# Two blocks on one core: narrower products in three passes, and the projections' first product begun inside the norms

## The reference, cut to what matters

```python
# block 1 (16 learned tokens in front: 1040 rows)
u = rms_norm(h, norm1_g)
a, bv, bg, q, k, v, fg, gates = split(u @ w_in)        # 256, 256, 256, 512, 512, 512, 8, 3*1024 columns
ya = pool_mixer(a) @ w_out_a                           # 256 deep
yb = conv_module(bv, bg) @ w_out_b                     # 256 deep
logf = log_sigmoid(fg + b_forget)                      # the "forget" product, 8 columns
yc = forgetting_attention(q, k, v, logf) @ w_out_c     # 512 deep
g = sigmoid(gates.reshape(B, L, 3, D))
merged = g[:, :, 0] * ya + g[:, :, 1] * yb + g[:, :, 2] * yc
h = h + merged @ w_o                                   # then a mixture of experts

# block 2
u = rms_norm(h, norm_mix_g)
x_rnn, g_rnn, q_c, kv_c, k_pe, gates = split(u @ w_in) # k_pe: 32 columns
xa = causal_conv(x_rnn)
r = sigmoid(blockwise(xa, wa) + ba); i = sigmoid(blockwise(xa, wx) + bx)   # four blocks of 256 x 256 each
ya = scan(a(r), b(i, xa)) * gelu(g_rnn)
yb = mla(q_c, kv_c, k_pe, positions)                   # latent attention
h = h + (gates_0 * ya + gates_1 * yb) @ w_out          # then another mixture of experts
```

## Time and profile before

| | before |
|---|---|
| runs (us) | 2941.87, 2947.04, 2951.19: median 2947.04 |
| the profiled execution | 2947.81; span of its trace 2946.0 |
| PE busy | 2662.0 us, 90% of the span, 12234 matmuls |
| DVE, ACT, POOL busy | 1487.1, 1113.0, 826.2 us (50%, 38%, 28%) |
| mean granted clock of PE | 0.954 |

### The profile page before, as it was taken

The page is one execution under the profiler, slowest core; times in us unless marked ns, Lnnn a source line. Parts: engine busy times, 40 slices in busy tenths (PEclk is TensorE's granted clock), DMA queues, the critical chain, the costliest instruction groups (busy, mean ns, idle before and its releaser), DMA issues. The chain is left out here.

```text
span 2946.0 us, 34212 instructions
## 1 busy us (share of the span) xinstructions
PE 2662.0 (90%) x12234; PEld 2032.9 (69%) x12234; DVE 1487.1 (50%) x1840; ACT 1113.0 (38%) x1461; POOL 826.2 (28%) x685
## 2 busy tenths in 40 slices
PE   4999899999999799958999799999999999699887
PEld 3899565776768677736777455557777868677665
DVE  4196343222223478855476544433542542678775
ACT  3011443000012277752344344441332232377775
POOL 1243332212112133412100233232333322144545
PEclk9999899999999799968899899999999999799999
DMA  3110112111105487842522232322111223598995
GB/s 95 30 51 22 33 43 58 41 50 43 43 18 184 168 290 235 277 127 82 214 65 65 75 85 73 74 74 81 43 42 50 57 88 125 193 326 301 325 316 195
DMA packets 209416, 350.52 MB, mean 119 GB/s; under 512 B 40376, under 2 KB 159496, under 8 KB 189608
## 3 DMA queue, kind: packets, MB, share of 16 engines
q1 hardware_dynamic: 191824, 315.60, 32.2%
q0 software_dynamic: 17280, 33.60, 4.9%
q10 hardware_dynamic: 216, 0.07, 0.0%
HBM read 326.80 MB, written 72.48 MB: 136 GB/s over the span
## 5 line engine op out<-in xcount | busy, mean ns | idle before, releaser
L2101 DVE TENSOR_TENSOR moe_run_w_low_up<-moe_run_w,moe_run_w_high_up 128x2048 fp32r<-128x2048 f32 x116 | 265.4, 2290 | 123.0 <-ACT moe_run_w_high_up L1934 122.7
L1934 ACT CAST moe_run_w_high_up<-moe_run_w 128x2048 fp32r<-128x2048 f32 x116 | 221.2, 1907 | 117.1 <-DMA moe_run_w<-w_gate 59.2
L1871 PE MATMUL moe_run_up<-moe_run_w_high_up,moe_run_xT_high 128*128 128x512 f32 x464 | 193.0, 416 | 21.0 <-issue 20.7
L1871 PE MATMUL moe_run_up<-moe_run_w_high_up,moe_run_xT_low 128*128 128x512 f32 x464 | 184.3, 397 | 0.0
L1871 PE MATMUL moe_run_up<-moe_run_w_low_up,moe_run_xT_high 128*128 128x512 f32 x464 | 184.2, 397 | 0.0
L1417 DVE TENSOR_TENSOR merge_gated<-merge_branch,merge_gate 128x512 f32<-128x512 f32 x48 | 33.2, 692 | 281.1 <-ACT merge_gate L1401 280.9
L1277 ACT ACTIVATE mla_probs<-mla_scores 128x512 f32<-128x512 f32 x192 | 94.1, 490 | 177.5 <-PE mla_scores L1209 91.8
L1401 ACT ACTIVATE merge_gate<-merge_gates 128x512 f32<-128x512 f32 x48 | 28.7, 598 | 348.0 <-PE merge_branch L122 348.0
L1222 PE MATMUL mla_out<-mla_probs,mla_v 128*65 128x512 f32 (+3 forms) x384 | 151.2, 489 | 0.0
L2101 DVE TENSOR_TENSOR moe_run_w_low_down<-moe_run_w,moe_run_w_high_down 128x2048 fp32r<-128x2048 f32 x58 | 132.4, 2282 | 0.0
L1296 DVE TENSOR_REDUCE mla_piece_max<-mla_max 128x1 f32<-128x512 f32 (+1 forms) x192 | 99.0, 550 | 62.8 <-PE mla_max L1181 42.9
(11 more groups left out here) (570 smaller groups left out, 7394.2 us busy)
## 6 DMA issues: line engine op xcount, KB each, us to landing
moe_run_w<-exp_w SPq DMA_DIRECT2D x72, 1024.0 KB
moe_run_w<-w_gate SPq DMA_DIRECT2D x34, 1024.0 KB
moe_run_w<-w_up SPq DMA_DIRECT2D x34, 1024.0 KB
moe_run_w<-w_down SPq DMA_DIRECT2D x34, 1024.0 KB
out_h<-x SPq DMA_DIRECT2D x16, 512.0 KB
v<-out_v SPq DMA_DIRECT2D x16, 512.0 KB, 2.9
mla_raw_q_then_weights<-w_in SPq DMA_DIRECT2D x16, 512.0 KB, 3.9
rnn_raw<-w_in SPq DMA_DIRECT2D x16, 512.0 KB
```

The lines of the kernel that those rows point to most:

```text
L1871: last = pe.matmul(up[p][:], a, w, start=(h == 0 and k == 0), stop=(h == 1 and k == 3 * HK - 1))
L1934: act.copy(hi[p][j], raw[p][j][:]).then_inc(s_hi[j], 1)
L2101: dve.tensor_tensor(lo[p][j], raw[p][j][:], hi[p][j].bitcast(F32), ALU.subtract).then_inc(s_lo[j], 1)
```

## The change

Four edits.

1. *merge1*: the products of the second and third branch are made in three passes. For this ACT casts the six feature slices to high parts and DVE subtracts the low ones at the start of the stage (the last slice in two halves, behind `hand.s_out`), and POOL splits the branch weights in each `m`. Their raw forms and low parts share memory, so a block is loaded only when PE has used the block before; SP's order changes with it. Two sigmoid buffers serve three branches.
2. *rnn*: the block matrices' products are made in three passes, POOL splits `wr` and `wi` for each `q`, DVE splits `xa`.
3. *norms*: a `FirstProduct` object moves the first piece of the forget product (norm1) and of the rotated key's (norm3) into the norm, six matmuls behind the transposes of each of the tiles 4 to 7. POOL splits their weights there, and the first two column blocks of the projection are loaded there.
4. *accumulators*: DVE and ACT give their counts first thing in the projection (`banks_free`).

The diff, cut:

```diff
+class FirstProduct:
+    def __init__(self, nc, mem, name, raw, uT, cols, w, c0, runs):
...
+        self.w = [sb(f"w_{n}", [P, KD, self.n], F32R) for n in ("high", "low")]
+        self.next_raw = [sb(f"next_raw{p}", [P, KD, P], F32) for p in range(2)]
...
+    def load_next(self, sp, s_next):
+        for dst, src in zip(self.next_raw, self.next_src):
+            sp.dma_start(dst[:], src).then_inc(s_next, 16)
+
+    def step(self, pe, k):
+        a, b = self.cols
+        (wh, wl), (uh, ul) = self.w, self.uT
+        out = self.acc[0:self.n, 0:b - a]
+        pe.matmul(out, wh[:, k, :], uh[:, k, a:b], start=(k == 0), stop=False)
+        pe.matmul(out, wh[:, k, :], ul[:, k, a:b], start=False, stop=False)
+        pe.matmul(out, wl[:, k, :], uh[:, k, a:b], start=False, stop=(k == KD - 1))
...
+                begun.load_next(sp, s_next)
...
+            @block.gpsimd
+            def _(pool):
+                own = Steps(pool, st.sem("pool_step"))
+                pool.wait_ge(s_pre, 16 * len(prefetch))
+                split(pool, own, begun.raw[:], begun.w[0][:], begun.w[1][:]).then_inc(s_begun, 1)
...
+                    if t == begun.TILES:
+                        pe.wait_ge(s_begun, 1)
+                        pe.wait_ge(s_low, 2 * begun.TILES)
+                    if t >= begun.TILES:
+                        k = begun.PER_TILE * (t - begun.TILES)
+                        for c in range(k, min(k + begun.PER_TILE, KD)):
+                            begun.step(pe, c)
...
+                    sp.sem_inc(s_raw[p], 16)
+                done = 1
+                for r, (f, o, n) in enumerate(runs):
+                    skip = 1 if r == 0 else 0
+                    with sp.Fori(0, n // 2 - skip) as i:
+                        for p in range(2):
+                            at = (2 * i + (f + 2 * skip)) * P + (c0 + P * p)
+                            sp.wait_ge(s_w[p], i + (done + 1))
+                            sp.dma_start(raw[p][:], src[:, :, bass.ds(at, P)]).then_inc(s_raw[p], 16)
...
+            def banks_free(eng, e):
+                if parts:
+                    eng.sem_inc((s_rest, s_square)[e], PER)
+                else:
+                    for p in range(2):
+                        eng.sem_inc(s_free[e][p], share[e])
+
             def copy_out(eng, e):
-                for p in range(2):
-                    eng.sem_inc(s_free[e][p], share[e])
...
-                act.sem_inc(s_square, PER)
...
-                dve.sem_inc(s_rest, PER)
...
+                banks_free(dve, 0)
...
+                banks_free(act, 1)
...
-            pe.wait_ge(s_w, 1)
+            pe.sem_inc(s_acc, 1)
             for n, (a, b) in enumerate(PIECES1):
+                if n == 0:
...
-            split(dve, own, raw[:], wb[0][:], wb[1][:]).then_inc(s_w, 1)
...
+                                         (f"{name}_spare{n}", [P, BANK], F32R)) for n in range(2)))
         self.sums = [sb(f"sums{n}", [P, BANK // P], F32) for n in range(2)]
...
                     for b in range(NB):
...
-                            sp.wait_ge(s_split, u + 1)
...
+                        if m:
+                            sp.wait_ge(s_gy, NU * (m - 1) + NB + b + 1)
+                        if m or b:
+                            sp.dma_start(raw[b], gsrc[b, :, :, at]).then_inc(s_raw[b], 16)
+                        sp.dma_start(wy_raw[b][:], chunked(outs[b])[:, :, at]).then_inc(s_wy[b], 16)
...
-                pool.sem_inc(s_split, 3)
-                for u in range(1, NB * KD):
-                    pool.wait_ge(s_raw[u % 2], 16 * ((u + 1) // 2))
-                    pool.wait_ge(s_gy, NU * (u // NB + 1) + NB + u % NB + 1)
-                    split(pool, own, raw[u % 2], wg[u % NB][0][:], wg[u % NB][1][:]).then_inc(s_split, 1)
+                pool.sem_inc(s_split, 1)
+                for m in range(KD):
+                    for b in range(NB):
+                        if m or b:
+                            pool.wait_ge(s_raw[b], 16 * m + 16 * min(b, 1))
+                            split(pool, own, raw[b], *wg[b]).then_inc(s_split, 1)
+                        if b:
+                            pool.wait_ge(s_wy[b], 16 * m + 16)
+                            split(pool, own, wy_raw[b][:], wy[b][0][:], wy[b][1][:]).then_inc(s_wys, 1)
...
+                with pe.Fori(0, KD) as m:
+                    for h, (a, z) in enumerate(HALVES):
+                        for b in range(NB):
+                            pe.wait_ge(s_done, NU * m + NB * h + b + 1)
+                            if h == 0:
+                                pe.wait_ge(s_split, NB * m + b + 1)
+                            split_products(pe, ps_g[b][:], [([w[:, k, :] for w in wg[b]], uT(k, a, z))
+                                                            for k in range(KD)])
-                                if b == NB - 1:
-                                    pe.wait_ge(hand.s_out, 2 * heads)
-                                products(pe, ps_y[b][:], [(wy[p][:, starts[b] + k, :], of(k, a, z))
-                                                          for k in range(n)]).then_inc(s_gy, 1)
+                                    pe.wait_ge(s_wy[0], 16 * m + 16)
+                                last = products(pe, ps_y[0][:], [(wy_raw[0][:, k, :], plain(k, a, z))
+                                                                 for k in range(kk[0])])
+                            else:
+                                at = sum(kk[1:b])
+                                if h == 0:
+                                    pe.wait_ge(s_wys, (NB - 1) * m + b)
+                                pe.wait_ge(s_low, kk[1] if b == 1 else len(pieces))
+                                last = split_products(pe, ps_y[b][:], [([w[:, k, :] for w in wy[b]],
+                                                                        [high(at + k, a, z), lows[at + k][:, a:z]])
+                                                                       for k in range(kk[b])])
+                            last.then_inc(s_gy, 1)
...
-                            act.activation(sg[u % NB][:], ps_g[u % NB][:], ACT.Sigmoid).then_inc(s_sg, 1)
+                for k, a, z in pieces:
+                    if k == NR - 1 and a == 0:
+                        act.wait_ge(hand.s_out, 2 * heads)
+                    act.copy(high(k, a, z) if k == NR - 1 else highs[k][:], raws[k][:, a:z]).then_inc(s_high, 1)
...
+                        h, b = divmod(u, NB)
+                        act.wait_ge(s_gy, NU * m + u + 1)
+                        act.wait_ge(s_add, 4 * m + 2 * h + (2 if b == NB - 1 else 1))
+                        act.activation(sg[min(b, 1)][:], ps_g[b][:], ACT.Sigmoid).then_inc(s_sg, 1)
...
+                for n, (k, a, z) in enumerate(pieces):
+                    if k == NR - 1 and a == 0:
+                        finish[1](dve)
+                    dve.wait_ge(s_high, n + 1)
+                    dve.tensor_tensor(lows[k][:, a:z], raws[k][:, a:z],
+                                      (high(k, a, z) if k == NR - 1 else highs[k][:]).bitcast(F32),
+                                      ALU.subtract).then_inc(s_low, 1)
                 dve.sem_inc(s_done, NB)
...
+                            g = NU * m + NB * h + b
+                            gate = sg[min(b, 1)][:]
+                            dve.wait_ge(s_sg, g + 1)
+                            dve.tensor_tensor(gate, ps_y[b][:], gate, ALU.mult).then_inc(s_done, 1)
+                            dve.wait_ge(s_done, g + 1 + NB)
+                            if b:
+                                dve.wait_ge(s_add, 4 * m + 2 * h + b)
+                                dve.tensor_tensor(dst if b == NB - 1 else sg[0][:], sg[0][:], sg[1][:],
+                                                  ALU.add).then_inc(s_add, 1)
...
+        aa, xa_low = over(nc, st.ctx, ("rnn_a", [P, NCH, S], F32), ("rnn_xa_low", [P, NCH, S], F32R))
+        gm, xa_high = over(nc, st.ctx, ("rnn_gate_1", [P, NCH, S], F32), ("rnn_xa_high", [P, NCH, S], F32R))
...
+                    if j == NW - NCH:
+                        if q == 0:
+                            pool.wait_ge(hand.s_out, 2 * H2)
+                        pool.wait_ge(s_wl, 32 * q + 32)
+                        for n in range(2):
+                            split(pool, own, wl[n][:], wl_high[n], wl_low[n][:]).then_inc(s_wls, 1)
...
-                    pe.wait_ge(s_wl, 32 * q + 32)
-                    pe.wait_ge(s_xa, NCH * q + 2 * NCH)
+                    pe.wait_ge(s_wls, 2 * q + 2)
+                    pe.wait_ge(s_xl, NCH * q + NCH)
...
-                                products(pe, ps[u % RING][:], [(wl[n][:, k, c * P:(c + 1) * P], xa[:, k, a:b])
-                                                               for k in range(NCH)]).then_inc(s_ps, 1)
+                                split_products(pe, ps[u % RING][:],
+                                               [([w[n][:, k, c * P:(c + 1) * P] for w in (wl_high, wl_low)],
```

(6 more changed lines are left out.)

177 lines of the change are left out of this document (85 added, 92 removed).

## The result

The changed kernel takes 2911.19 us (median of 6 runs, 2909.74 to 2915.97), the kernel before 2947.15 (6 runs, 2941.87 to 2956.01): the ratio is 0.9872, with a 95% interval of 0.9858 to 0.9885, so 36 us or 1.3% faster. 2904 was predicted, and 2911 lies in the range. The number was better than its reasons, though: one cost of 16 us was not seen, and two gains were underestimated by half of that together.

A forecast was written before the change was run, and what follows sets the result against it. PE, busy in 90% of the span, was taken as the bound, with its waits at the seams. Savings of 15.9 + 0.7 + 10.3 + 12.4 + 4.2 = 43.5 us from 2947.8 gave 2904.3, said as 2904, range 2891 to 2917.

The forecast's parts named there:

- Merge, the passes: merge1: three passes replace f32 products in the second and third branch, 0.99 us saved 16 times, −15.9 us.
- The covers: merge1: weight loads and POOL's splits hide behind PE's two other units, 14.2 us at least, with about 7 us of slack.
- Merge, the start: Start of merge1: feature splits end about 515.5, PE wants the last at 520.7; 5 us of slack, no cost.
- The slower side's mechanism: merge1: gate weights' single raw buffers, loads landing over 11 us after issue hold PE; 13 us eats 43.5; chance 0.03.
- no wait of PE above 1.5 us: Sign for merge1: PE shows no longer wait, and the stage is near 367 us.
- Merge, the order of the loads: merge1: branch 1's gate weights, loaded second instead of fourth, shorten PE's 1.55 us wait, −0.7 us.
- norm1 and proj1: First product in norm1 at half rate, stage ending 2.9 us later, early counts starting proj1's columns at 58.0: −12.4 us.
- the rival of the clock: Clock rises in the norms: 5.2 us more gained in proj1, 4.4 in proj2, total 2894.5 us; chance 0.25.
- norm3 and proj2: First product's matmuls in norm3 at half rate; proj2's columns start at 1350.5 instead of 1354.68, −4.2 us.
- a clock of 1.00 in norm3: Sign in norm3: 1.00 would show the clock rising in the norms; the forecast expected still 0.50.
- The rule: Norms: transposes don't count as busy for PE's clock as matmuls do, so it stays low; the clock decides 9 us.
- rnn: rnn: 48 passes in about 11.1 us replace f32 products of 13.73, in four blocks, −10.3 us (−10.0 to −10.5).

The follow-up runs named there:

- count_first: The changed kernel with DVE's count of free accumulators in merge1 given first, ahead of the feature splits and finish: 2898.31 us, ratio 0.9827.
- count_mid: The changed kernel with DVE's count in merge1 placed behind the first five feature slices, ahead of finish: 2906.91 us, ratio 0.9864.
- merge_old: The changed kernel with the merge stage of the kernel before (second and third branch in plain f32, its buffers and orders): 2912.24 us, ratio 0.9883.
- counts_late: The changed kernel with both projections' accumulator counts given behind the forget and rotated key's chains again, as before the change: 2932.20 us, ratio 0.9945.
- product_out: The changed kernel with the first piece of the forget and rotated key's products back at the start of the projections: 2925.96 us, ratio 0.9919.
- loads_late: The changed kernel with the projections' first two column blocks loaded at the start of the projection instead of in the norm: 2919.41 us, ratio 0.9894.
- transposes_in_place: product_out with nine further transposes of the identity, output unused, behind tiles 4 to 7 of both norms where six matmuls stood: 2923.94 us, single run.
- rnn_old: The changed kernel with the rnn stage of the kernel before (block matrices in plain f32, their splits gone): 2918.11 us, ratio 0.9895.
- seam_filled: count_first with twenty further transposes of the identity, output unused, on PE at the end of norm1: 2902.04 us, ratio 0.9829.
- second_piece: count_first with the forget product's second piece in norm1 as well, 24 matmuls in a second accumulator: 2895.53 us, ratio 0.9817.
- count_first_again: count_first run once more, unchanged, beside seam_filled and second_piece on one chip: 2894.11 us, ratio 0.9816.

## Why the prediction was right, and where it was not

**Merge, the passes: right.** −15.9 predicted; with the count first merge1 is 15.2 us shorter than with the stage of before in the same program (386.52 − 371.28). The covers held as worked out: nothing of POOL's new splits or of the single buffers shows as a wait of PE.

**Merge, the start: wrong, by 16 us.** The step is "At the stage's start ACT and DVE split six feature slices ... 5 us of slack, nothing". It asked when PE needs what the slices give, and what is queued on ACT behind the wait for `finish`, and answered both rightly. It did not ask what is queued on DVE behind the same wait: the count `s_done`, which stood ahead of `finish` before and stands behind it now. The line is in the diff, as context that did not change; its surroundings did. The slower side's mechanism was not this one either. Count_first and count_mid show the cause twice over, by 16.35 and 11.9 us of the stage. Of the prediction's signs, "no wait of PE above 1.5 us" is the one that failed by it.

**Merge, the order of the loads: −0.7 said, nothing shown.** With the new order PE waits 0.46 and 0.75 us for branch 1's gate weights (count_first and its repetition), with the old one 0.60 (merge_old). POOL can begin the split earlier, 8.0 and 8.9 us behind the attention's last product instead of 9.6, but it then falls beside DVE's subtractions and takes longer (last section).

**norm1 and proj1: the mechanism right, the size wrong.** −12.4 predicted, −16.15 measured. Tiles were taken as 3.72 us apart, PE as the norm's new bound, and the stage as ending 2.9 late. The clock rose in the norm, and the stage ended in time: DVE's first row of proj1 stands at 44.61, not at 48.1. It was the rival of the clock for the norm; but its "columns start at 52.8" wasn't reached either, since the clock fell again in the seam, which that rival had not considered: 54.35 measured, 58.0 and 52.8 said. The early counts gave 10.7 us, 8.2 of it waiting (counts_late), the product in the norm 4.2 (product_out), the loads in the norm 0.1 (loads_late).

**norm3 and proj2: likewise.** −4.2 predicted, −8.26 measured, and the rival said −8.6. Here the clock was up behind the seam, and proj2's first 24 matmuls ran at the full rate. The rival's own sign, a clock of 1.00 in norm3, did not come: 0.59 was measured, since it rose only in the tiles with the added work and fell once in between.

**The rule.** The row was read rightly, and the conclusion drawn from it was too wide. The clock at 0.50 belongs to a PE that had 15.75 us of transposes in 49.30, not to transposes as such. The Trainium skill, page "TensorE: Matmul & The Clock Gate", section "Part 4: PE-mode transpose", says that the raised clock does not engage for them. The run of transposes_in_place does not agree: transposes alone, f32 ones of 128 x 128, brought themselves from 1.97 to 1.04 us for eight. The page's example is bf16, which no run here shows; for the f32 ones the measurement decides.

**rnn: right.** −10.3, measured −9.62 between the two profiles and 10.65 by rnn_old.

**The sum.** The additions hold; only the clock rival's total comes to 2894.7 by its own terms (2904.3 − 5.2 − 4.4), not 2894.5. −43.5 was said, and the stages' measured changes that answer to its terms are −16.2, −0.2, −8.3 and −9.6, −34.2. The missed cost (+16) and the two gains that came out 7.8 larger (3.7 and 4.1) nearly make up the difference. That the total came out near was luck: the forecast's 2904.3 with the missed 16 alone would be 2920, outside the range, and with the two gains alone 2896.5; the two errors happened to offset each other.

## What to carry to other kernels

When work is put at the head of an engine's program, read on to what that engine hands out behind it: a count given by a bare increment costs nothing by itself, and cost 16 us here when a wait was put ahead of it. Give counts of free buffers first. And work for TensorE in the idle gaps of a stage can be worth more than its own time if the clock is then up at the start of the next one: in proj2 it was, behind gaps of 1.32 to 1.72 us, in all eleven profiles with the added work, matmuls or transposes; in proj1, behind 3.2 to 3.5 us, it fell at once or a few matmuls later in nine of them, and stayed up in seam_filled and second_piece, where the gap was 1.35 and 2.68. The first branch in three passes too would, at 0.33 us 16 times, give some 5 us more by this estimate; it needs memory for two more slices of high parts and wasn't tried.

## What the runs showed of the hardware that was not expected

- f32 transposes alone lift TensorE's granted clock: in transposes_in_place eight took 1.97 us at 27.96 and 1.04 at 34.33, with nothing but transposes between.
- The length of one idle gap of PE does not tell whether the clock falls behind it. It was still up behind 1.32 us (changed kernel), 1.35 (seam_filled), 2.28 (loads_late) and 2.68 (second_piece). Behind 2.39 us at the start of merge1 in merge_old seven matmuls ran at the half rate at once; behind 2.59 us there in count_first six ran at the full rate and then eight at the half; behind 2.35 us in norm3 of the changed kernel it fell after 1.4 us of work; and behind 3.35 us there were 17 matmuls at the half rate. From the timeline of merge_old:

```profile
476.17 0.79 PE L134 MATMUL merge_gates<-uT_high,fox_q_hi_then_high 128*128 128x512 f32 x1 [2.39 <-DVEq L1460]
...
476.75 0.63 PE L134 MATMUL merge_gates<-uT_low,fox_q_hi_then_high 128*128 128x512 f32 x1
```

- A semaphore increment on DVE that stands alone runs ahead of the arithmetic in front of it: in count_mid PE had the count 2.6 us before DVE's subtractions ended.
- POOL's split of a block, 1.04 + 2.34 us otherwise, took 1.86 + 3.20 in merge1 of the changed kernel, where both parts were begun while DVE subtracted f32 slices, until 488.80. In count_first_again DVE was through at 486.73, and the subtraction that POOL began behind that took 2.35:

```profile
485.87 1.86 POOL L146 CAST merge_wg_high<-merge_raw 128x1024 fp32r<-128x1024 f32 x1 [6.12 <-DMA merge_raw<-w_in]
...
487.80 3.20 POOL L147 TENSOR_TENSOR merge_wg_low<-merge_raw,merge_wg_high 128x1024 fp32r<-128x1024 f32 x1
```

From the timeline of count_first_again:

```profile
487.71 2.35 POOL L147 TENSOR_TENSOR merge_wg_low<-merge_raw,merge_wg_high 128x1024 fp32r<-128x1024 f32 x1
```
